# ScalarE, in place of SyncE, begins the transfers that turn x between the stages

## The reference

```
for l in range(DEPTH):
    x = x + 0.5 * swiglu_ffn(rmsnorm(x, norm_ffn1[l]), w_ffn1_in[l], w_ffn1_out[l])
    u = rmsnorm(x, norm_mix[l])
    proj = u @ w_in[l]
    q, k, v, g, p, c, gates = jnp.split(proj, split_points, axis=-1)
    y_ret = (retention(q, k, v, positions) * jax.nn.silu(g)) @ w_ret_out[l]
    y_pool = pool_mixer(p, w_pool[l], pool_scale[l])
    y_conv = conv_module(c, conv_w[l], conv_b[l], conv_ln_g[l], conv_ln_b[l], w_conv_out[l])
    gates = jax.nn.sigmoid(gates + gate_bias[l]).reshape(B, S, N_BRANCHES, D)
    merged = gates[:, :, 0] * y_ret + gates[:, :, 1] * y_pool + gates[:, :, 2] * y_conv
    x = x + merged @ w_out[l]
    x = x + 0.5 * swiglu_ffn(rmsnorm(x, norm_ffn2[l]), w_ffn2_in[l], w_ffn2_out[l])
return rmsnorm(x, norm_final)
```

## Time and profile before

| | us |
|---|---|
| three timed runs | 1126.18, 1126.68, 1126.96 (median 1126.68) |
| the profiled execution, its own time | 1126.8 |
| its span, first to last instruction | 1125.0 |
| PE busy in the span | 1118.0 (99%) |
| DVE busy | 801.8 (71%) |
| ACT busy | 650.2 (58%) |

### The profile page before, as it was taken

The page is one execution under the profiler, slowest core; times in us unless marked ns, Lnnn a source line. Parts: engine busy times, 40 slices in busy tenths (PEclk is TensorE's granted clock), DMA queues, the critical chain, the costliest instruction groups (busy, mean ns, idle before and its releaser), DMA issues.

```text
span 1125.0 us, 13064 instructions
## 1 busy us (share of the span) xinstructions
PE 1118.0 (99%) x5006; PEld 925.1 (82%) x5006; DVE 801.8 (71%) x985; ACT 650.2 (58%) x744; POOL 39.0 (3%) x68
## 2 busy tenths in 40 slices
PE   9999999999999999999999999999999999999997
PEld 7888888888888888888888888888888888888886
DVE  6856566899998875655476655378999987665553
ACT  7755546664657765554475554376637477756442
POOL 0100000000200100000000000000002001000000
PEclk9999999999999999999999999999999999999999
DMA  9996665763756786656597666467638677967551
GB/s 356 312 271 210 215 234 182 267 202 126 254 214 194 213 293 208 212 197 223 151 307 238 211 200 229 170 218 248 197 122 276 229 196 226 268 217 224 159 187 38
DMA packets 130862, 244.65 MB, mean 217 GB/s; under 512 B 99040, under 2 KB 100448, under 8 KB 106224
## 3 DMA queue, kind: packets, MB, share of 16 engines
q1 hardware_dynamic: 128016, 236.61, 64.3%
q0 software_dynamic: 1648, 6.06, 1.5%
q10 hardware_dynamic: 1136, 1.15, 0.3%
HBM read 219.16 MB, written 1.05 MB: 196 GB/s over the span
## 4 chain that ended last, share of the span: by engine, by line
PE 98%; DVE 1%; DMA 1%; ACT 0%; issue 0%; POOLq 0%; POOL 0%; DVEq 0%
PE acc L419 31%; PE acc L421 31%; PE acc L420 31%; PE acc L463 1%; PE acc L468 1%; DMA hT_planes<-h_planes 1%; PE acc L472 1%; PE ret L686 0%; DVE w_lo L1250 0%; PE tr L606 0%; PE tr L513 0%; DVE hT_whole L1295 0%; PE tr L598 0%; PE ret L618 0%; PE ret L620 0%; PE tr L596 0%
## 5 line engine op out<-in xcount | busy, mean ns | idle before, releaser
L1250 DVE TENSOR_TENSOR w_lo<-raw,w_hi 128x2048 fp32r<-128x2048 f32 (+2 forms) x204 | 445.6, 2215 | 84.6 <-ACT w_hi L819 84.4
L819 ACT CAST w_hi<-raw 128x2048 fp32r<-128x2048 f32 (+2 forms) x204 | 375.2, 1849 | 217.5 <-PE acc L421 209.6
L419 PE MATMUL acc<-w_hi,xT_hi 128*128 128x512 f32 x1152 | 450.9, 391 | 0.1
L421 PE MATMUL acc<-w_hi,xT_lo 128*128 128x512 f32 x1152 | 448.4, 389 | 0.0
L420 PE MATMUL acc<-w_lo,xT_hi 128*128 128x512 f32 x1152 | 448.3, 389 | 0.0
L419 PEld LDWEIGHTS acc<-w_hi,xT_hi 128*128 128x128 f32 x1152 | 216.3, 188 | 45.3 <-DVE w_lo L1250 0.9
L421 PEld LDWEIGHTS acc<-w_hi,xT_lo 128*128 128x128 f32 x1152 | 216.3, 188 | 45.2
L420 PEld LDWEIGHTS acc<-w_lo,xT_hi 128*128 128x128 f32 x1152 | 216.4, 188 | 44.0
L1333 DVE SCALAR_TENSOR_TENSOR h<-acc,rs,silu_gate 128x256 f32<-128x256 f32 x88 | 42.5, 483 | 154.2 <-ACT silu_gate L886 154.2
L419 PE MATMUL acc<-w_hi,hT_hi 128*128 128x512 f32 x348 | 135.4, 389 | 0.0
L420 PE MATMUL acc<-w_lo,hT_hi 128*128 128x512 f32 x348 | 135.4, 389 | 0.0
(11 more groups left out here) (144 smaller groups left out, 657.1 us busy)
## 6 DMA issues: line engine op xcount, KB each, us to landing
raw<-in_weights SPq DMA_DIRECT2D x192, 1024.0 KB, 5.0
raw<-in_weights SPq DMA_DIRECT2D x20, 256.0 KB, 5.8
raw<-in_weights SPq DMA_DIRECT2D x8, 512.0 KB, 3.4
bias<-in_gate_bias POOLq DMA_DIRECT2D x6, 512.0 KB, 6.5
x<-in_x SPq DMA_DIRECT2D x2, 512.0 KB, 10.8
scale_row<-in_pool_scale POOLq DMA_DIRECT2D x2, 512.0 KB, 6.8
hT_planes<-h_planes SPq DMA_TRANSPOSE x54, 3.1
band<-in_band POOLq DMA_DIRECT2D x1, 768.0 KB, 7.0
```

Of the source, the lines that this page charges most:

```text
L419: nc.tensor.matmul(o, a_hi, b_hi, start=first, stop=False)
L421: return nc.tensor.matmul(o, a_lo, b_hi, start=False, stop=last)
L819: nc.scalar.copy(w_hi[:, hf % HIGHS, 0:n], raw[:, hf % RAWS, 0:n]).then_inc(hi_split, 1)
L1250: nc.vector.tensor_tensor(w_lo[:, hf % RAWS, 0:n], raw[:, hf % RAWS, 0:n], w_hi[:, hf % HIGHS, 0:n].bitcast(F32), ALU.subtract).then_inc(l ...
```

## The change

In `split_x`, ACT itself waits for its copy and begins the transpose of the piece, with the same two waits that SP had. `turn_x` and its calls are gone from SP's list. Nothing else is changed: the same 20 transposes, in the same order, of the same tiles, now on ACT's DMA queue.

```diff
-            def turn_x(l, norm, t, c):
-                at = piece(l, norm, t, c)
-                sp.wait_ge(x_split, at + 1)
-                if at > 1:
-                    sp.wait_ge(x_joined, at - 1)
-                sp.dma_start_transpose(xT_planes[c][:].rearrange("p a (g n) -> p (a g) n", n=P),
-                                       x_planes[c].rearrange("p a k n -> p (a k n)")
-                                       ).then_inc(x_turned[c], 16)
...
-                for at, norm in ((0, 0), (MIX, 1), (FFN2, 3)):
-                    if (hf // HALVES, norm) in SEAM:
-                        for ahead, t, c in ((2, 0, 0), (2, 0, 1), (3, 1, 0), (3, 1, 1)):
-                            if hf % HALVES == 2 * at + ahead:
-                                turn_x(hf // HALVES, norm, t, c)
...
                 nc.scalar.copy(x_planes[c],
                                x[:, t, columns(c)].bitcast(U16)
                                .rearrange("p (k n a) -> p a k n", k=4, a=2)).then_inc(x_split, 1)
+                at = piece(l, norm, t, c)
+                act.wait_ge(x_split, at + 1)
+                if at > 1:
+                    act.wait_ge(x_joined, at - 1)
+                act.dma_start_transpose(xT_planes[c][:].rearrange("p a (g n) -> p (a g) n", n=P),
+                                        x_planes[c].rearrange("p a k n -> p (a k n)")
+                                        ).then_inc(x_turned[c], 16)
```

## The result

The changed kernel takes 1158.34 us in the median of four runs (1156.33 to 1160.09), beside 1126.72 for the kernel before: a ratio of 1.028, interval 1.0267 to 1.0292. It is 31.6 us slower. The forecast was 1131.0 with a range of 1126.6 to 1139.5, so the sign was right and the size far off. The profiled execution took 1160.09 us, its span is 1158.3, and its mean granted clock is 0.987. Against the span of before, 33.3 us have to be found.

A forecast was written before the change was run, and what follows sets the result against it. PE, busy 99% of the span, was taken to bound the kernel. Three stalls of 0.4 us and two of 1.65 made 4.5, less 0.24, 4.3: 1131.1 on the profiled 1126.8, 1131.0 in the median, range 1126.6 to 1139.5.

The forecast's parts named there:

- What bounds the kernel, and no gain from SP: Whole kernel: PE is busy 99% of the span; SP's waits were for ACT's copy, so an earlier transpose wins at most 0.24 us.
- The cost on ACT: In the seams: each transpose issue takes ACT 1.23 us, making the cast of half hf + 3 2.4 or 2.8 us late.
- The 0.4 in three seams and 1.65 in two: PE stalls before a stage's 37th matmul: 0.4 us in seams after a feed-forward, 1.65 after a mixer, 4.5 together.
- What SP gains is hidden, and can do harm: In the seams: three loads go earlier, winning nothing, and run beside the t = 1 transposes; landing taken as up to 4.4 us.
- it decides from 4.7: At t = 1: a landing up to 4.7 us costs nothing, since the cast holds DVE's subtraction until 748.05.
- the parameters' 12.2 us: Upper bound for a landing: ACT's 160 KB of parameters took 12.2 us beside SP's loads; left out, as only two loads interfere.
- The rival of contention: In five seams: t = 1 transposes share engines with loads, land after 6.8 us, stall 2.45 each; 1138.7 us, chance 0.30.
- 0.24: Before layer 1's second feed-forward: the hole of 0.24 us between two PE matmuls already in the profile before, subtracted from the stalls.
- More than all this: Rival, in the seams: contention and a longer issue together, as ACT may not finish its second issue meanwhile; chance 0.05.
- The signs named beforehand: Profile after: PE holes of 0.4 or 1.65 us, SP's transpose waits gone, three loads begun by 742.2; landings over 4.7 mean contention.
- the walk: Main case: ACT's order followed through both kinds of seam, DVE's subtraction late behind the cast; 1129.0 to 1133.0 us, chance 0.45.

The follow-up runs named there:

- the square was out of the way: The kernel with the short hold, with ACT's square of t = 0 moved behind the cast of half hf + 3: 1135.29 us, ratio 1.0076.
- the one with loads right behind the issue: Short hold with the square moved, but SP's loads wait for ACT's one-column copy behind its second issue, not the first t = 1 landing: 1130.49 us.
- the kernel with PE kept busy: The changed kernel with 16 matmuls of no use per seam ahead of the wait for half hf + 3: 1149.54 us, ratio 1.0211.
- the kernel with the short hold: The changed kernel, with SP holding each seam's three loads until the first t = 1 transpose has landed: 1141.55 us, ratio 1.0133.

## Why the prediction was wrong

*What bounds the kernel, and no gain from SP.* Right. PE waited for nothing, so there was nothing to win, and SP's waits at the transposes were no queueing.

*The cost on ACT.* Right in mechanism and near in size. The 1.23 us per issue was 1.25. The 0.4 in three seams and 1.65 in two were 0.63 and 1.8 where the loads were held for the shorter time, so the sum of 4.5 us was 5.5 by the starts of the matmuls; the idle time there, 4.7, fell to 1.3 once the square was out of the way. In the changed kernel this delay is hidden behind a longer one.

*What SP gains is hidden, and can do harm.* This is the step that failed. The prediction saw that the loads would run beside the t = 1 transposes, called the landing the unknown, and took the lower side, up to 4.4 us, where it decides from 4.7. It was 7.3 to 9.2 for the first of the two. In the seams of before no load was in flight when a transpose began, and the three loads came 1.27 us or more behind the start of the last one, because SP's list held them back until both were issued. That list was not an accident of queueing but a gate. The experiment with the loads on ACT and the transposes on SP shows that losing the gate is enough for the whole loss; the one with loads right behind the issue shows that restoring it takes away most.

The trace of before had a nearer row than the parameters' 12.2 us, outside the seams. In layer 1's second feed-forward a transpose was begun at 966.38, 3.1 us or more behind the starts of two loads of SP's own queue that had not landed:

```profile
hT_planes<-h_planes SPq DMA_TRANSPOSE x1, 7.1
```

That is one queue and not two, but a transpose behind loads had taken 7.1 us there, well over the 4.7 from which the landing decides.

*The rival of contention* (0.30) had the mechanism, and two terms too small. It drained the loads by 749.2, at 5.0 + 2.1 us for the last of them, and so had the transposes at 6.8. But the loads took longer than that beside the transposes: in the seam shown the last load, begun at 760.94, landed at 769.68, after 8.7 us, and the first transpose landed at 770.65, 9.2 us after its start. Its stall of 2.45 was 3.8 to 5.0, and five of them 22.2 us in place of 12.2. It also counted PE's lost time as the idle time alone. The clock behind the five holes took another 11.4 us by the counts, 7 to 11 by the kernel with PE kept busy; this term stood in no case of the prediction. 1126.8 + 22.2 + 11.4 - 0.24 is 1160.2, and the profiled execution took 1160.09.

*The rule on packets.* The Trainium skill, "DMA: Bandwidth & Descriptors", section "Queues, rings and completion order", says that an engine takes turns between its queues a packet at a time, a packet being some 9 to 17 descriptors, and my estimate by it was a landing of 4.0 to 4.8 us. The turns agree with the trace and the size of a turn does not. The two transposes of the seam shown went as 2112 packets of the profile for 0.52 MB, some 250 bytes each, so 66 packets of one transpose on each of 16 engines, where the estimate had 64 descriptors in 4 to 7 turns. The loads' 3.67 MB went in 512 packets, some 7 KB each. Where both queues had work for some time, they moved one packet each in turn, as far as the counts tell: in the kernel with the short hold, from 760 to 764 us,

```profile
q1 hardware_dynamic: 200, 1.52, 90.7%
q10 hardware_dynamic: 199, 0.05, 5.4%
```

So every small packet lets a large one pass, and the loads drain first. The changed kernel fits this in the seam shown. From 761.48, the start of the first transpose's issue, to 765 the loads' queue moved 164 packets and the transposes' none; from 769.5, when the last load was done or nearly so, to 771.6 the transposes' queue moved 1513 and the loads' none:

```profile
q1 hardware_dynamic: 164, 1.18, 100.2%
```

```profile
q10 hardware_dynamic: 1513, 0.37, 85.8%
```

These 1513 are most of the transposes' 2112 packets. No run varied the size of the packets, so that it is the cause is argued and not shown, and turns alone don't explain why no packet of the transposes moved before 765.

*More than all this* (0.05) named the longer second issue. It came, 3.2 to 5.5 us, but with the transposes on SP it cost ACT nothing and the time was the same, so it is a companion of the late landing and, as far as these two runs tell, not a second price.

*The signs named beforehand.* The hole's releaser was DVE's subtraction, as the walk had it, but that waited for the join behind a DMA, as contention had it; the landings were over 4.7 us. SP's waits at the transposes are gone, and the last freed load began at 760.94, 0.5 us ahead of DVE's last addition, as foreseen from the earlier trace rows.

*What stays open:* what makes the issuer wait during a second issue, and why the second seam was hit harder than the others with the short hold (12.3 and 12.5 us, with its loads at 11.4 and more). For the second the traces have a companion. In both kernels one transfer of the instruction queue, q8, fell into that landing, and none into the late landings of the other three seams. In the first of them, from 388 to 401 us:

```profile
q8 instruction: 1, 0.02, 0.6%
xT_planes<-x_planes ACTq DMA_TRANSPOSE x1, 12.3
```

From 391 to 394 us the loads' queue and the transpose's moved 0.08 MB together. No run moved that transfer, so that it is the cause is not shown.

## What to carry to other kernels

A transfer that stands in an in-order list of transfers also holds back what is behind it; before it is moved to another engine, ask which transfers it was keeping off the DMA engines, and whether a small transfer on the critical path will then share them with large ones. A landing that was measured alone is no price for that transfer in company. And a wait of PE of several us has to be priced with the clock behind it.

## What was not expected of the hardware

- A DMA transpose of 128x1024 16-bit numbers that lands in 3.0 us alone took 7.3 to 9.6 us as the first t = 1 transpose of a seam in the changed kernel and in the one with the loads on ACT, where two or three loads of 1 MB were in flight when it began. It took 7.7 to 12.5 us where three were begun 0.64 us behind its start, but 3.1 to 3.2 where they were begun 1.3 to 1.5 us behind it.
- The issuer of the second transpose was held for 3.2 to 6.2 us in these two kernels while the first one was late, on ACT's queue and on SP's.
- Where loads and a transpose had work for 4 us, their queues moved 200 and 199 packets, though those of the loads were some 7.6 KB and those of the transpose some 250 bytes.
- With the holes of 3.8 to 5.0 us in PE the granted clock fell to 1.2 GHz, in the hole or within 0.5 us of its end, and stayed there for 3.4 to 6.8 us; with matmuls in the hole it stayed at 2.4. Behind six holes of 2.1 to 2.4 us in kernels that held loads back it fell four times.
